# GpSimd's 1024 gathers of expert rows: a loop with copied lists of four ids, and one gather after the other that reads its own column of ids

## The chip, the cores and the metric

The kernel runs on one core of one Trainium2 chip. Its time is the device time of one launch in microseconds (us). Engines are named PE (TensorE, matmuls; PEld is its weight load), DVE (VectorE), ACT (ScalarE), POOL (GpSimd) and SP (SyncE, which only issues DMAs here). All DMAs, those of SP and those of POOL, run on the core's 16 DMA engines.

## The reference, cut to what matters

A decoder trunk of two layers on 256 tokens of 1024 numbers, all in float32. Each layer has a mixer (gated linear attention in layer 0, attention with forget gates in layer 1) and then a feed-forward part that looks up experts:

```python
def peer_ffn(xn, w_pq, sub_keys, u_tab, v_tab):
    q = einsum('td,de->te', xt, w_pq).reshape(T, 8, 2, 128)
    s = einsum('thcd,hcnd->thcn', q, sub_keys)
    s_top, i_top = lax.top_k(s, 16)
    cand = s_top[:, :, 0, :, None] + s_top[:, :, 1, None, :]
    best, pos = lax.top_k(cand, 16)             # 8 heads x 16 experts for each token
    ids = ...                                   # number of an expert, 0 to 16383
    gates = softmax(best)
    u = take(u_tab, ids)                        # one row of 1024 numbers each
    a = gelu(einsum('cd,chkd->chk', x, u))
    v = take(v_tab, ids)
    out = einsum('chk,chkd->cd', gates * a, v)
```

So every token needs 128 rows of the table u and 128 rows of the table v in each layer. With 256 tokens and 2 layers that is 2 x 2 x 128 gathers of u (one row for each of 128 tokens, 512 KB) and as many of v: 1024 gathers.

## The kernel before, in words

The tokens are two tiles (b = 0, 1) of 128, a token in each partition. A **phase** is the expert work of one layer and one tile; there are four, in the order (layer 0, tile 0), (0, 1), (1, 0), (1, 1). Each engine has one program, written out by hand, and semaphores join them. The mixers and the routing of the next phase are put between the experts of the phase that runs, in a fixed order on each engine.

The expert rows pass through two rings of SBUF, `u_ring` and `v_ring`, with 8 slots each (`RING`). A **round** fills both rings once, so a phase has 16 rounds, and a round has two **halves** of four slots. POOL issues an indirect DMA for each slot (L522 for u, L539 for v). It reads one id in each partition and fetches the row with this number.

For every u slot DVE multiplies the row with the token and sums it up (L796, a custom operation of two inputs, 128x1024), and so frees the slot (`u_free`). For a half ACT then computes the gelu (L1099), the weights (L1104) and for six of the eight slots a diagonal matrix (L1112). PE multiplies this diagonal with the v row and adds it up in PSUM (L1501, two matmuls of 128x512 a slot, `v_free`). The other two slots of v (2 and 3) are added by DVE (L806, `vec_free`).

SP loads the weights of the mixers and of the routing in blocks of 1 MB, nearly all into two places that take turns. A place can be loaded again only when PE has multiplied its last block (`w_used`). PE works in order: if it waits for a block of weights, the diagonals of the next experts wait behind that.

POOL's own program, after some constants, is the loop over rounds. In the function `turn` it takes four slots at a time (`ISSUE`): it waits until all four slots of u are free, copies the four ids of each token from `ids` to the small list `u_ids` (L516), waits for this copy (`ids_laid`) and issues four gathers of u; then the same for v with `v_ids` (L533). The loop's register picks the ids, while the gathers read at fixed addresses. A quarter of a phase (four rounds) begins when DVE has routed its two heads (`routed`).

Of the kernel before, what the change touches and what calls it, by code (L numbers as in the profile page):

```python
# [7 lines left out]
U32 = mybir.dt.uint32  # L8
# [5 lines left out]
P = 128  # L14
# [12 lines left out]
SLOTS = RH * RTOP  # L27

RING = 8
SUB = 4  # L30
ISSUE = 4
ROUNDS = SLOTS // RING
VEC_SLOTS = [2, 3]
PE_SLOTS = [j for j in range(RING) if j not in VEC_SLOTS]
VEC = len(VEC_SLOTS)
QUARTER = ROUNDS // 4
HALVES = ROUNDS * RING // SUB
LAST_VEC = RING - 3
PHASES = [(layer, b) for layer in range(2) for b in range(TILES)]
# [175 lines left out]
def yoco_kernel(nc, a, out):  # L215
# [9 lines left out]
    with ExitStack() as ctx:  # L225
        def sb(name, shape, dt=F32):
            return ctx.enter_context(nc.sbuf_tensor(name, shape, dt))

        def sem(name):
            return ctx.enter_context(nc.semaphore(name))  # L230
# [9 lines left out]
        u_ring = sb("u_ring", [P, RING, D])  # L240
        v_ring = sb("v_ring", [P, RING, D])
# [49 lines left out]
        ids = sb("ids", [P, TILES, SLOTS], U32)  # L291
# [1 line left out]
        gate_e = sb("gate_e", [P, SLOTS])  # L293
        gate_sum = sb("gate_sum", [P, RH])
        gate_inv = sb("gate_inv", [P, RH])
        u_ids = sb("u_ids", [P, RING], U32)
        v_ids = sb("v_ids", [P, RING], U32)
        dots = sb("dots", [P, RING])
        gelus = sb("gelus", [P, RING])
        weights_s = sb("weights_s", [P, RING])  # L300
# [48 lines left out]
        pv_full = sem("pv_full")  # L349
        queryT_full, queryT_ready = sem("queryT_full"), sem("queryT_ready")  # L350
        gate_x_ready, gate_e_ready, routed = sem("gate_x_ready"), sem("gate_e_ready"), sem("routed")
        ids_laid = sem("ids_laid")
        issued = sem("issued")
        u_loaded = [sem(f"u_loaded{j}") for j in range(RING)]
        v_loaded = [sem(f"v_loaded{j}") for j in range(RING)]

        u_free, v_free, vec_free = sem("u_free"), sem("v_free"), sem("vec_free")
# [33 lines left out]
        def multiplied(key):  # L391

            return w_used, RELEASE_OF[key] + 1
# [70 lines left out]
        def _(pool):  # L464
# [40 lines left out]
            u_rows = a["peer_u"].rearrange("l n d -> (l n) d")  # L505
            v_rows = a["peer_v"].rearrange("l n d -> (l n) d")

            def turn(ph, b, r, waits=None):

                for j0 in range(0, RING, ISSUE):  # L510
                    numbers = ids[:, b, bass.ds(r * RING + (j0 - ph * SLOTS), ISSUE)]
                    slots = range(j0, j0 + ISSUE)
                    n_laid = 2 * (j0 // ISSUE)
                    pool.wait_ge(u_free, r * RING + (j0 + ISSUE))
                    pool.sem_inc(issued, 1)
                    nc.gpsimd.tensor_copy(u_ids[:, j0:j0 + ISSUE], numbers).then_inc(ids_laid, 1)  # L516
                    if waits:
                        pool.wait_ge(*waits[n_laid])
                    pool.wait_ge(ids_laid, r * (2 * RING // ISSUE) + (n_laid + 1))
                    pool.sem_inc(issued, 1)  # L520
                    for j in slots:
                        pool.indirect_dma_start(  # L522
                            u_ring[:, j, :], None, u_rows, bass.IndirectOffsetOnAxis(ap=u_ids[:, j:j + 1], axis=0)
                        ).then_inc(u_loaded[j], 16)
                    on_pe = sum(j < j0 + ISSUE for j in PE_SLOTS)
                    on_dve = sum(j < j0 + ISSUE for j in VEC_SLOTS)
                    if any(j in PE_SLOTS for j in slots):
                        pool.wait_ge(v_free, r * len(PE_SLOTS) + on_pe)
                        pool.sem_inc(issued, 1)
                    if any(j in VEC_SLOTS for j in slots):  # L530
                        pool.wait_ge(vec_free, r * VEC + on_dve)
                        pool.sem_inc(issued, 1)
                    nc.gpsimd.tensor_copy(v_ids[:, j0:j0 + ISSUE], numbers).then_inc(ids_laid, 1)  # L533
                    if waits:
                        pool.wait_ge(*waits[n_laid + 1])
                    pool.wait_ge(ids_laid, r * (2 * RING // ISSUE) + (n_laid + 2))
                    pool.sem_inc(issued, 1)
                    for j in slots:
                        pool.indirect_dma_start(  # L539
                            v_ring[:, j, :], None, v_rows, bass.IndirectOffsetOnAxis(ap=v_ids[:, j:j + 1], axis=0)  # L540
                        ).then_inc(v_loaded[j], 16)

            for ph, (layer, b) in enumerate(PHASES):
                for quarter in range(4):
                    pool.wait_ge(routed, ph * 4 + quarter + 1)
                    first = ph * ROUNDS + quarter * QUARTER
                    if first == 0:

                        turn(0, 0, 0, [multiplied(key) for key in ((("wo", 0, 0), 2), ("r", 1),
                                                                   (("pq", 0, 0), 5), (("pq", 0, 0), 7))])  # L550
                    with pool.Fori(max(first, 1), first + QUARTER) as r:
                        turn(ph, b, r)


        @block.vector
# [1186 lines left out]
```

## Time and profile before

| what | value |
|---|---|
| median of 3 runs | 1933.5 us (1932.65 to 1946.42) |
| span of the profiled execution | 1954.8 us |
| instructions in it | 17629 |
| moved by DMA | 621.46 MB, of it 536.94 MB by the gathers |
| mean granted clock of PE | 0.835 of full speed |

The page of the profile gives no time of the profiled execution but its span, from the first instruction to the last, and the end of the output's DMA lies in it. The span is 21.3 us above the median of the runs and 8.4 us above the slowest of them. So an amount of time is taken off the span, and the difference is then carried over to the median.

To read it: time in which an engine is busy says what it does, and the waits say for whom. Where POOL neither works nor waits for another engine, the page puts the gap down to "issue". A gather's duration on POOL is the time in which POOL writes its descriptors; the rows land later, some 6 us after the issue.

### The profile page before, as it was taken

The page shows a single profiled execution, that of the slowest core. Times are in us where ns is not written, and L with a number is a line of the kernel's source. Part 1 is how long each engine was busy: PE and PEld are TensorE (multiplying, and loading weights), DVE is VectorE, ACT ScalarE, POOL GpSimd, SP SyncE. Part 2 cuts the span into 40 slices and gives each one's busy share as a digit, 9 for nine tenths or more (in the row PEclk, how much of TensorE's full clock was granted, in tenths as well). Part 3 has the DMA queues.
Part 4 walks back from the last instruction along what each step waited for, and adds up shares of the span by engine and source line. Part 5 has one row for each costly group of instructions (what it writes and reads, how often), then busy time and mean ns, then how long its engine had stood idle before and what let it go on. Part 6 is the DMA issues. An engine that isn't in the chain of part 4 may idle for free.

```text
span 1954.8 us, 17629 instructions
## 1 busy us (share of the span) xinstructions
PE 1344.8 (69%) x4795; PEld 799.3 (41%) x4800; DVE 1101.8 (56%) x2324; ACT 480.6 (25%) x1341; POOL 1239.8 (63%) x1317
## 2 busy tenths in 40 slices
PE   7997665566646868676846787698875766655554
PEld 6885322233313645444523454465442433222221
DVE  3336976544756539353574754834456588544445
ACT  3212233222212213242221212233122122211111
POOL 2007777775777755477577774745667777777774
PEclk9999887787878979878878898888887887878776
DMA  8459998999999997799998999977998999989997
GB/s 286 135 179 322 359 327 307 310 338 380 330 322 371 346 389 277 276 340 336 352 341 313 328 392 327 344 263 270 335 349 313 341 315 336 323 303 333 331 325 254
DMA packets 230275, 621.46 MB, mean 318 GB/s; under 512 B 21412, under 2 KB 97188, under 8 KB 230200
## 3 DMA queue, kind: packets, MB, share of 16 engines
q0 software_dynamic: 147456, 536.94, 76.3%
q1 hardware_dynamic: 82744, 83.62, 13.0%
q8 instruction: 36, 0.59, 0.1%
q14 instruction: 39, 0.32, 0.0%
HBM read 619.43 MB, written 1.05 MB: 317 GB/s over the span
## 4 chain that ended last, share of the span: by engine, by line
POOL 32%; issue 20%; PE 15%; DMA 14%; DVE 7%; ACT 2%; POOLq 1%; DVEq 0%; SPq 0%; ACTq 0%; PEldq 0%
POOL v_ring L539 16%; POOL u_ring L522 13%; PE acc L1501 8%; DMA u_ring<-in_peer_u,u_ids 4%; DVE u_ring L796 3%; DMA narrow<-in_kv_w 3%; PE pair L1350 3%; DMA wbuf<-in_fox_w_q 3%; DMA wbuf<-in_fox_w_o 2%; DVE h L806 2%; PE pair L1339 2%; POOL u_ids L516 1%; DMA wbuf<-in_gla_w_o 1%; DMA wbuf<-in_kv_w 1%; POOL v_ids L533 1%
## 5 line engine op out<-in xcount | busy, mean ns | idle before, releaser
L1501 PE MATMUL acc<-v_ring,diag 128*128 128x512 f32 x1524 | 826.5, 700 | 464.2 <-ACT diag L1112 462.5
L796 DVE CUSTOM_DVE_ANT_0 u_ring<-u_ring,xn 128x1024 f32<-128x1024 f32 x512 | 612.3, 1223 | 524.7 <-DMA u_ring<-in_peer_u,u_ids 520.6
L539 POOL DMA_INDIRECT v_ring<-in_peer_v,v_ids x512 | 598.3, 1169 | 223.2 <-issue 121.0
L1501 PEld LDWEIGHTS acc<-v_ring,diag 128*128 128x128 f32 x1524 | 334.3, 227 | 911.4 <-issue 618.5
L522 POOL DMA_INDIRECT u_ring<-in_peer_u,u_ids x512 | 540.8, 1056 | 225.8 <-issue 121.2
L1099 ACT ACTIVATE gelus<-dots 128x4 f32<-128x4 f32 x128 | 26.3, 205 | 865.1 <-DVE dots L796 864.7
L806 DVE SCALAR_TENSOR_TENSOR h<-v_ring,weights_s,h 128x1024 f32<-128x1024 f32 x128 | 164.4, 1284 | 32.2 <-ACT weights_s L1104 26.0
L1350 PE MATMUL pair<-wbuf,xT 128*128 128x256 f32 x352 | 98.1, 444 | 54.2 <-DMA wbuf<-in_kv_w 25.1
L516 POOL COPY u_ids<-ids 128x4 uint32 (+1 forms) x128 | 49.4, 386 | 126.8 <-DVE gates L737 126.1
L1112 ACT ACTIVATE diag<-ident,weights_s 128x128 f32<-128x128 f32 x381 | 125.3, 391 | 6.8
L533 POOL COPY v_ids<-ids 128x4 uint32 (+1 forms) x128 | 37.6, 294 | 120.3 <-PE acc L1501 110.9
L1099 ACT ACT_TABLE_LOAD x42 | 53.9, 1283 | 244.0 <-DVE dots L796 243.9
L1104 ACT ACTIVATE weights_s<-gelus,gates 128x1 f32<-128x1 f32 x512 | 109.0, 283 | 8.3 <-ACT gelus L1099 3.1
L1350 PEld LDWEIGHTS pair<-wbuf,xT 128*128 128x128 f32 x352 | 78.4, 227 | 75.9 <-DMA wbuf<-in_kv_w 28.0
L1339 PE MATMUL pair<-xT,wbuf 128*128 128x128 f32 (+2 forms) x528 | 79.6, 318 | 32.1 <-DMA wbuf<-in_fox_w_q 31.0
L1339 PEld LDWEIGHTS pair<-xT,wbuf 128*128 128x128 f32 (+1 forms) x528 | 73.4, 211 | 41.6 <-DMA wbuf<-in_fox_w_q 33.0
L1421 PEld LDWEIGHTS pair<-xT,wbuf 128*128 128x128 f32 x768 | 87.5, 192 | 6.3 <-issue 4.9
L1421 PE MATMUL pair<-xT,wbuf 128*128 128x128 f32 x768 | 87.8, 275 | 1.1 <-ACT xT L1032 1.1
L665 DVE TENSOR_TENSOR h<-h,pair 128x1024 f32<-128x1024 f32 x4 | 4.9, 1222 | 67.1 <-PE pair L1350 67.1
L796 DVE DVE_READ_ACCUMULATOR2_ANT dots<- 128x1 f32 x512 | 42.1, 82 | 0.0
L580 DVE SCALAR_TENSOR_TENSOR rows<-h,rstd,pair 128x1024 f32<-128x1024 f32 x4 | 5.1, 1281 | 55.1 <-PE pair L1405 55.0
L763 DVE TENSOR_REDUCE neg_max<-pair 128x2 f32<-128x256 f32 (+1 forms) x16 | 8.9, 558 | 46.7 <-PE pair L1458 46.6
(192 smaller groups left out, 1063.0 us busy)
## 6 DMA issues: line engine op xcount, KB each, us to landing
wbuf<-in_peer_w_q SPq DMA_DIRECT2D x20, 1024.0 KB, 14.9
wbuf<-in_kv_w SPq DMA_DIRECT2D x10, 1024.0 KB, 20.5
u_ring<-in_peer_u,u_ids POOLq DMA_INDIRECT x512, 6.2
v_ring<-in_peer_v,v_ids POOLq DMA_INDIRECT x512, 6.1
wbuf<-in_fox_w_q SPq DMA_DIRECT2D x8, 1024.0 KB, 16.6
wbuf<-in_fox_w_o SPq DMA_DIRECT2D x8, 1024.0 KB, 11.3
wbuf<-in_gla_w_o SPq DMA_DIRECT2D x6, 1024.0 KB, 15.0
wbuf<-in_gla_w_in SPq DMA_DIRECT2D x4, 1024.0 KB, 8.3
```

Source lines behind the costliest of these rows:

```text
L516: nc.gpsimd.tensor_copy(u_ids[:, j0:j0 + ISSUE], numbers).then_inc(ids_laid, 1)
L522: pool.indirect_dma_start(u_ring[:, j, :], None, u_rows, bass.IndirectOffsetOnAxis(ap=u_ids[:, j:j + 1], axis=0)).then_inc(u_loaded[j], 16)
L539: pool.indirect_dma_start(v_ring[:, j, :], None, v_rows, bass.IndirectOffsetOnAxis(ap=v_ids[:, j:j + 1], axis=0)).then_inc(v_loaded[j], 16)
L796: nc.vector.tensor_tensor_reduce(out=u_ring[:, j, :], in0=u_ring[:, j, :], in1=xn[:, b, :], scale=1.0, scalar=0.0, op0=ALU.mult, op1=ALU.a ...
L806: nc.vector.scalar_tensor_tensor(out=h[:, b, :], in0=v_ring[:, jv, :], scalar=weights_s[:, jv:jv + 1], in1=h[:, b, :], op0=ALU.mult, op1=A ...
L1099: nc.scalar.activation(gelus[:, s], dots[:, s], ACT.Gelu).then_inc(dots_free, 1)
L1104: ins = nc.scalar.activation(weights_s[:, j:j + 1], gelus[:, j:j + 1], ACT.Copy, scale=gates[:, b, bass.ds(r * RING + (j - ph * SLOTS), 1)])
L1112: nc.scalar.activation(diag[:, k, :], ident[:, :], ACT.Copy, scale=weights_s[:, j:j + 1]).then_inc(diag_ready, 1)
L1339: ins = nc.tensor.matmul(dst(m // P, mm), w[:, c, m:m + mm], x[:, c], start=(c == 0), stop=(c == KC - 1))
L1350: ins = nc.tensor.matmul(dst[:, i // 2, (i % 2) * WCOLS:(i % 2 + 1) * WCOLS], x[:, c, :], w[:, c, :], start=(c == 0), stop=(c == KC - 1))
L1421: ins = nc.tensor.matmul(dst[:, 0, o:o + P], w[:, c, m * P:(m + 1) * P], xT[:, slot, c, :], start=(c == 0), stop=(c == KC - 1))
L1501: ins = nc.tensor.matmul(acc[:, i, :], diag[:, k, :], v_ring[:, j, i * HALF:(i + 1) * HALF], start=False, stop=False)
```

## The change

Each of the 1024 gathers now stands by itself in POOL's program. Its ids come straight from a column of `ids` at a fixed address. The copies, the lists `u_ids` and `v_ids`, their semaphore and the loop are gone. Each gather waits for its own slot, where the loop waited for four slots at once. The order stays: four of u, four of v.

```diff
--- before.py
+++ after.py
@@ -28,7 +28,6 @@
 
 RING = 8
 SUB = 4
-ISSUE = 4
 ROUNDS = SLOTS // RING
 VEC_SLOTS = [2, 3]
 PE_SLOTS = [j for j in range(RING) if j not in VEC_SLOTS]
@@ -293,8 +292,6 @@
         gate_e = sb("gate_e", [P, SLOTS])
         gate_sum = sb("gate_sum", [P, RH])
         gate_inv = sb("gate_inv", [P, RH])
-        u_ids = sb("u_ids", [P, RING], U32)
-        v_ids = sb("v_ids", [P, RING], U32)
         dots = sb("dots", [P, RING])
         gelus = sb("gelus", [P, RING])
         weights_s = sb("weights_s", [P, RING])
@@ -349,7 +346,6 @@
         pv_full = sem("pv_full")
         queryT_full, queryT_ready = sem("queryT_full"), sem("queryT_ready")
         gate_x_ready, gate_e_ready, routed = sem("gate_x_ready"), sem("gate_e_ready"), sem("routed")
-        ids_laid = sem("ids_laid")
         issued = sem("issued")
         u_loaded = [sem(f"u_loaded{j}") for j in range(RING)]
         v_loaded = [sem(f"v_loaded{j}") for j in range(RING)]
@@ -505,51 +501,44 @@
             u_rows = a["peer_u"].rearrange("l n d -> (l n) d")
             v_rows = a["peer_v"].rearrange("l n d -> (l n) d")
 
-            def turn(ph, b, r, waits=None):
-
-                for j0 in range(0, RING, ISSUE):
-                    numbers = ids[:, b, bass.ds(r * RING + (j0 - ph * SLOTS), ISSUE)]
-                    slots = range(j0, j0 + ISSUE)
-                    n_laid = 2 * (j0 // ISSUE)
-                    pool.wait_ge(u_free, r * RING + (j0 + ISSUE))
-                    pool.sem_inc(issued, 1)
-                    nc.gpsimd.tensor_copy(u_ids[:, j0:j0 + ISSUE], numbers).then_inc(ids_laid, 1)
-                    if waits:
-                        pool.wait_ge(*waits[n_laid])
-                    pool.wait_ge(ids_laid, r * (2 * RING // ISSUE) + (n_laid + 1))
-                    pool.sem_inc(issued, 1)
-                    for j in slots:
-                        pool.indirect_dma_start(
-                            u_ring[:, j, :], None, u_rows, bass.IndirectOffsetOnAxis(ap=u_ids[:, j:j + 1], axis=0)
-                        ).then_inc(u_loaded[j], 16)
-                    on_pe = sum(j < j0 + ISSUE for j in PE_SLOTS)
-                    on_dve = sum(j < j0 + ISSUE for j in VEC_SLOTS)
-                    if any(j in PE_SLOTS for j in slots):
-                        pool.wait_ge(v_free, r * len(PE_SLOTS) + on_pe)
+            def u_group(ph, g):
+
+                b = PHASES[ph][1]
+                r, first = divmod(g * SUB, RING)
+                for j in range(first, first + SUB):
+                    at = r * RING + j - ph * SLOTS
+                    pool.wait_ge(u_free, r * RING + (j + 1))
+                    pool.indirect_dma_start(
+                        u_ring[:, j, :], None, u_rows, bass.IndirectOffsetOnAxis(ap=ids[:, b, at:at + 1], axis=0)
+                    ).then_inc(u_loaded[j], 16)
+
+            def v_group(ph, g):
+
+                b = PHASES[ph][1]
+                r, first = divmod(g * SUB, RING)
+                for j in range(first, first + SUB):
+                    at = r * RING + j - ph * SLOTS
+                    if j in VEC_SLOTS:
+                        pool.wait_ge(vec_free, r * VEC + (VEC_SLOTS.index(j) + 1))
+                    else:
+                        pool.wait_ge(v_free, r * len(PE_SLOTS) + (PE_SLOTS.index(j) + 1))
+                    pool.indirect_dma_start(
+                        v_ring[:, j, :], None, v_rows, bass.IndirectOffsetOnAxis(ap=ids[:, b, at:at + 1], axis=0)
+                    ).then_inc(v_loaded[j], 16)
+
+            for ph in range(len(PHASES)):
+                for g in range(ph * HALVES, (ph + 1) * HALVES):
+                    if g % (HALVES // 4) == 0:
+                        pool.wait_ge(routed, g // (HALVES // 4) + 1)
                         pool.sem_inc(issued, 1)
-                    if any(j in VEC_SLOTS for j in slots):
-                        pool.wait_ge(vec_free, r * VEC + on_dve)
+                    if g < 2:
+                        pool.wait_ge(*multiplied(((("wo", 0, 0), 2), (("pq", 0, 0), 5))[g]))
                         pool.sem_inc(issued, 1)
-                    nc.gpsimd.tensor_copy(v_ids[:, j0:j0 + ISSUE], numbers).then_inc(ids_laid, 1)
-                    if waits:
-                        pool.wait_ge(*waits[n_laid + 1])
-                    pool.wait_ge(ids_laid, r * (2 * RING // ISSUE) + (n_laid + 2))
-                    pool.sem_inc(issued, 1)
-                    for j in slots:
-                        pool.indirect_dma_start(
-                            v_ring[:, j, :], None, v_rows, bass.IndirectOffsetOnAxis(ap=v_ids[:, j:j + 1], axis=0)
-                        ).then_inc(v_loaded[j], 16)
-
-            for ph, (layer, b) in enumerate(PHASES):
-                for quarter in range(4):
-                    pool.wait_ge(routed, ph * 4 + quarter + 1)
-                    first = ph * ROUNDS + quarter * QUARTER
-                    if first == 0:
-
-                        turn(0, 0, 0, [multiplied(key) for key in ((("wo", 0, 0), 2), ("r", 1),
-                                                                   (("pq", 0, 0), 5), (("pq", 0, 0), 7))])
-                    with pool.Fori(max(first, 1), first + QUARTER) as r:
-                        turn(ph, b, r)
+                    u_group(ph, g)
+                    if g < 2:
+                        pool.wait_ge(*multiplied((("r", 1), (("pq", 0, 0), 7))[g]))
+                        pool.sem_inc(issued, 1)
+                    v_group(ph, g)
 
 
         @block.vector
```

In the order of POOL's program (row by row as it was compiled; ISA, REGISTER_ALU and the branch are steps of the sequencer) the body of the loop before reads, for the second half of a round and the end of the loop:

```order
L514 REGISTER_ALU
L516 ISA [waits u_free]
L516 COPY u_ids<-ids 128x4
L519 REGISTER_ALU
L522 DMA u_ring<-in_peer_u,u_ids 128x1024 [waits ids_laid]
L522 DMA u_ring<-in_peer_u,u_ids 128x1024 x3
L528 REGISTER_ALU
L533 COPY v_ids<-ids 128x4 [waits v_free]
L536 REGISTER_ALU
L539 DMA v_ring<-in_peer_v,v_ids 128x1024 [waits ids_laid]
L539 DMA v_ring<-in_peer_v,v_ids 128x1024 x3
```

One gather of four waits for a semaphore there, that of the copy. The changed program, at the beginning of a quarter of a phase, is:

```order
L511 DMA u_ring<-in_peer_u,ids 128x1024 [waits routed,u_free]
L511 DMA u_ring<-in_peer_u,ids 128x1024 [waits u_free] x3
L525 DMA v_ring<-in_peer_v,ids 128x1024 [waits v_free] x2
L525 DMA v_ring<-in_peer_v,ids 128x1024 [waits vec_free] x2
L511 DMA u_ring<-in_peer_u,ids 128x1024 [waits u_free] x4
L525 DMA v_ring<-in_peer_v,ids 128x1024 [waits v_free] x4
```

The gathers follow one another with nothing between them, and every one carries a wait for a slot. The programs of the other engines keep their instructions and their order.

## Rows read from the trace of the kernel before

**Rows 1.** The page, part 1: busy us, share, instructions of each engine.

```profile
PE 1344.8 (69%) x4795; PEld 799.3 (41%) x4800; DVE 1101.8 (56%) x2324; ACT 480.6 (25%) x1341; POOL 1239.8 (63%) x1317
```

**Rows 2.** POOL's groups by line: busy us, mean ns, idle before them and releasers.

```profile
L539 POOL DMA_INDIRECT v_ring<-in_peer_v,v_ids x512 | 598.3, 1169 | 223.2 <-issue 121.0 <-POOL v_ids L533 102.1
L522 POOL DMA_INDIRECT u_ring<-in_peer_u,u_ids x512 | 540.8, 1056 | 225.8 <-issue 121.2 <-POOL u_ids L516 103.1 <-PE acc L1501 1.5
L516 POOL COPY u_ids<-ids 128x4 uint32 (+1 forms) x128 | 49.4, 386 | 126.8 <-DVE gates L737 126.1
L533 POOL COPY v_ids<-ids 128x4 uint32 (+1 forms) x128 | 37.6, 294 | 120.3 <-PE acc L1501 110.9 <-DVE h L806 8.8
...
L498 POOL TENSOR_SCALAR_AFFINE_SELECT scratch<-scratch 128x128 f32<-128x128 f32 x7 | 4.5, 640 | 0.5
```

**Rows 3.** POOL in order of time: start us, us, what, idle before it.

```profile
1703.60 1.97 POOL L539 DMA_INDIRECT v_ring<-in_peer_v,v_ids  x1 [0.30 <-issue]
1705.57 0.39 POOL L516 COPY u_ids<-ids 128x4 uint32 x1
1706.77 0.96 POOL L522 DMA_INDIRECT u_ring<-in_peer_u,u_ids  x1 [0.81 <-POOL u_ids L516]
1708.03 0.94 POOL L522 DMA_INDIRECT u_ring<-in_peer_u,u_ids  x1 [0.30 <-issue]
```

**Rows 4.** DVE in order of time, beside the first of rows 3.

```profile
1703.54 1.22 DVE L796 CUSTOM_DVE_ANT_0 u_ring<-u_ring,xn 128x1024 f32<-128x1024 f32 x1
...
1704.69 1.22 DVE L796 CUSTOM_DVE_ANT_0 u_ring<-u_ring,xn 128x1024 f32<-128x1024 f32 x1
```

**Rows 5.** The line of u's gathers: durations in ns, least, median and most.

```profile
L522 POOL DMA_INDIRECT u_ring<-in_peer_u,u_ids x512: 935/941/1987, 143.5 to 1931.5; - x171
```

**Rows 6.** POOL's waits: us in total, times, longest us.

```profile
POOL v_ids L533 <- PE acc L1501: 110.9, 14, 20.3
```

**Rows 7.** The four phases: us, then PE, PEld, DVE, ACT, POOL busy, clock, DMA share, GB/s.

```profile
143.50:571.60 428.10, 268.38 (x866) 146.90 (x865) 271.61 (x576) 117.07 (x310) 304.93 (x320) 0.83 0.94 332
571.60:1047.00 475.40, 337.24 (x1264) 204.79 (x1265) 267.67 (x573) 121.30 (x354) 310.64 (x321) 0.83 0.92 335
1047.00:1524.50 477.50, 361.00 (x1359) 221.50 (x1360) 265.47 (x564) 119.91 (x338) 307.94 (x321) 0.84 0.90 325
1524.50:1938.40 413.90, 247.09 (x611) 114.25 (x612) 239.13 (x473) 79.22 (x273) 302.37 (x319) 0.80 0.92 325
```

**Rows 8.** The page, part 4: the chain that ended last, by engine.

```profile
POOL 32%; issue 20%; PE 15%; DMA 14%; DVE 7%; ACT 2%; POOLq 1%; DVEq 0%; SPq 0%; ACTq 0%; PEldq 0%
```

**Rows 9.** The chain in order of time: its longest pieces near where it leaves POOL.

```profile
394.68 5.25 DMA u_ring<-in_peer_u,u_ids
...
476.05 9.37 PE acc L1501 x16
...
657.36 5.58 DMA u_ring<-in_peer_u,u_ids
...
779.22 25.75 DMA wbuf<-in_fox_w_q
...
829.04 7.38 DMA u_ring<-in_peer_u,u_ids
...
1139.34 8.12 DMA u_ring<-in_peer_u,u_ids
```

**Rows 10.** The chain where it comes back to POOL.

```profile
817.46 1.17 POOL v_ids L533
```

**Rows 11.** POOL alone in the four stretches: us, busy (instructions), clock, share, GB/s.

```profile
394.70:485.60 90.90, 58.32 (x65) 0.79 0.98 357
657.40:817.50 160.10, 88.44 (x92) 0.85 0.89 325
829.00:956.60 127.60, 84.48 (x91) 0.80 0.97 348
1139.30:1434.70 295.40, 173.36 (x185) 0.84 0.89 323
```

**Rows 12.** Two windows of 50 us, columns as in rows 7.

```profile
200.00:250.00 50.00, 36.12 (x124) 20.16 (x124) 48.65 (x151) 12.25 (x34) 36.77 (x39) 0.86 0.97 353
600.00:650.00 50.00, 34.79 (x131) 19.95 (x130) 35.99 (x92) 13.79 (x33) 37.28 (x38) 0.83 1.03 391
```

## The prediction

> **What bounds the kernel now.** I read the busy shares first, then POOL's groups, POOL's rows in order of time, its waits, the windows of the four phases, and last the chain of waits. No engine is near full by the shares: PE has 69%, POOL 63%, DVE 56% [rows 1]. They mislead for POOL. Its gathers, copies and the gaps before them are 598.3 + 540.8 + 49.4 + 37.6 us of work and 223.2 + 225.8 us of gaps [rows 2], 1675 us in all, and the time from its first gather to its last is 1794.9 us (the sum of the four phases) [rows 7]. The gaps there are its own, "issue" or the wait for its own copy. What POOL waits for others is 110.9 us for PE in 14 places and 8.8 us for DVE (the 126.1 us for DVE's gates are the start, before the first gather) [rows 2, 6]. So outside of some 120 us POOL issues gathers as fast as it can, and the first question is how much of that is not gathering.
>
> The second question is where POOL matters for the end. The chain of waits gives POOL 32% and issue 20% of the span, and 38% to PE, DMA, DVE and ACT [rows 8]. In order of time the reader should see four long stretches in which the chain leaves POOL with a gather that lands, and goes through PE, DVE and blocks of weights, until PE frees a slot and POOL may go on: from 394.7 to 485.6, 657.4 to 817.5, 829.0 to 956.6 and 1139.3 to 1434.7 us [rows 9 to 11]. A block of weights alone is 25.75 us there [rows 9]. These are 674 us. In them POOL runs ahead of PE until its 8 slots are used up, and time saved on POOL is only waited out later. The other 1794.9 - 674 = 1121 us are led by POOL.
>
> **The change, part by part.** Work comes in 256 groups of four gathers (128 copies for u, 128 for v).
>
> *Removed: the copy.* On average it takes (386 + 294)/2 = 340 ns [rows 2].
>
> *Removed: the gap after the copy.* The gather behind it starts 0.81 us after its end. *Added in its place:* the gap between two gathers, 0.30 us [rows 3]. Together a group loses 0.34 + 0.81 - 0.30 = 0.85 us of about 6.5 us (1675/256), 217 us over all 256.
>
> *Added: a wait on every gather.* No row of before shows a gather that follows a gather and carries a wait. The bounds are 0.30 us (no wait, behind a gather) and 0.81 us (a wait, behind a copy) [rows 3]. I take 0.30. Semaphores by themselves are quick on POOL: the seven steps of L498, each of which waits for the one before, have 0.5 us of idle time together [rows 2], so most of the 0.81 is not the signal but the preparation of a gather that can't begin before the copy has ended. With a slot long free, nothing keeps the sequencer from preparing the next gather while the last one runs. Where the slot is not free the 0.81 appears, but the time is then PE's anyway.
>
> *Kept: the gather itself.* Its median is 0.94 us and its most 1.99 us [rows 5], with means of 1.169 and 1.056 [rows 2], so 0.17 us a gather come on top of the median. The row of 1.97 us lies under two operations of DVE that read two inputs each, and the one of 0.94 us at 1708 lies beside none [rows 3, 4]. I keep the 0.17, since DVE's work stays the same. The Trainium skill, "GPSIMD Engine Reference", section 1 (Specifications), says that POOL shares its interfaces to SBUF with VectorE and that instructions of VectorE with two SBUF inputs contend with it; by this rule the lengthening comes back with every gather, while one that came from full DMA queues would grow as POOL becomes faster. The rows fit the rule.
>
> *Removed: the loop, the waits for four slots at once.* The sequencer's steps run beside the gathers (the copy at 1705.57 starts right when the gather ends [rows 3]); I cost them at nothing. If that cover is missing it is a step of hundredths of a us each. A finer wait lets POOL start up to three slots earlier after a stall, at 14 places; PE then leads, and it gives nothing either.
>
> *Off and on the path.* In the four stretches POOL has 65 + 92 + 91 + 185 = 433 instructions, five to a group, 87 groups [rows 11]. Their 74 us become POOL's waits for PE. The other 169 groups lie on the path: 169 x 0.85 = 144 us. Two windows can't give their part. From 200 to 250 DVE is busy for 48.65 of 50 us (39/5 groups would save 6.6, at most 1.35 is there), and from 600 to 650 the DMA engines move 391 GB/s, the most of any window, with share 1.03 (6.5 us) [rows 12]. That leaves 144 - 5 - 7 = 132 us.
>
> **Sum.** 1954.8 - 132 = 1823 us for the span. The span is 21.3 us above the median of the runs; against that median of 1933.5 it is 1933.5 - 132 = 1801.5, so 1802 us. Its own range, from the unknown wait (0.36 us in place of 0.30 in half of the gathers is 30 us) and from stretches of PE that grow or shrink, is 1770 to 1835.
>
> What is late next: PE in the middle phases (337.24 of 475.4 us and 361.00 of 477.5 us busy [rows 7], 74% and 79% after the change), and the DMA engines elsewhere.
>
> **Rivals.**
>
> *All of it counts.* POOL's rows form a nearly closed line, and the chain may overstate PE: in the four stretches it is perhaps only just ahead, and the waits would stay at 120 us. Then all 217 us go: 1717 us. Against it speaks that the rings are only 8 slots deep and the chain does not touch POOL for up to 295 us [rows 11]. Chance 0.13, 1717 to 1770.
>
> *The DMA engines cap it.* In the last phase, with hardly any weights, they move 325 GB/s at a share of 0.92 [rows 7]; if the share can only go to 1, that is 353 GB/s. The last phase moves 413.9 x 325 = 134.5 MB, and needs 381 us, a gain of 33; the first moves 142.1 MB, 403 us, a gain of 25; the parts of the middle phases that POOL leads (188 and 182 us) gain 5%, 9 us each. Together 76 us: 1857 us. Against it: 391 GB/s over 50 us [rows 12]. For it: in that window a part are weights, and the share may count an idle wait as busy. Chance 0.18, 1835 to 1885.
>
> The Trainium skill, "DMA: Bandwidth & Descriptors", section Specifications, gives about 358 GB/s as a core's limit on HBM. With this figure the four gains would be 38, 31, 12 and 12 us, an estimate of 1840 us. The window of 391 GB/s stands against it as a limit for a core that runs alone.
>
> *Slower: each wait costs the long gap.* If 0.81 us belongs to any gather that carries a wait, and not to the copy, all 1024 have it. A gather is then 0.94 + 0.17 + 0.81 = 1.92 us, 1024 of them 1966 us, and POOL leads everywhere: with the 143.5 us before and the 16.4 us after them 2126 us of span, 2105 us as a median. It decides from a mean gap of 0.30 + 0.85/4 = 0.51 us upwards. For it: the only gathers with a wait have just this gap [rows 3]. Against it: the quick semaphores above. Chance 0.10, 1960 to 2110.
>
> *Nothing left.* Gathers that come sooner crowd the weights on the same 16 engines; if the blocks (25.75 us [rows 9]) take a third longer, the 674 us grow by what the rest gains. Chance 0.09, 1905 to 1960, in the main without a measurable difference. That the change does not do what it says is excluded by the compiled order: no copy is left between the gathers.
>
> **How the numbers follow.** My forecast has 0.50; with the cap (0.18) and all of it (0.13), faster by over 1% (1%, 19 us, is what a measurement of this kernel can tell) has 0.81. Same has 0.08 and slower 0.11, from the last two. The likeliest case gives 1802. The range has to hold 8 in 10: the forecast, the cap and most of the case above it, 1725 to 1890; outside are the two losing cases and the low end.
>
> **What would show it.** Right: gathers on POOL follow one another at 0.30 us, with means near 1.1 us; POOL's waits for PE grow from 111 to some 190 us; phases one and four shrink by about 40 and 50 us, the middle ones by 15 to 25 each; the windows of the last phase move about 370 GB/s. Wrong: a gap of 0.5 us or more before satisfied waits, gathers of 1.3 us in the mean without DVE beside them, a last phase that stays near 353 GB/s, or weights that land a third later.

## The result, and the profile after

The changed kernel takes 1799.3 us (median of 4 runs, 1787.6 to 1803.1), the kernel before 1933.1 us (4 runs on the same chip). The ratio is 0.928, with a 95% interval of 0.924 to 0.933: 134 us less. The forecast was 1802 us.

The page of the changed kernel, part 1 and part 4 (busy us by engine, then the chain that ended last):

```profile
PE 1304.0 (73%) x4800; PEld 789.3 (44%) x4800; DVE 1099.0 (61%) x2324; ACT 481.1 (27%) x1341; POOL 1167.7 (65%) x1061
...
PE 35%; POOL 21%; DMA 16%; DVE 16%; issue 9%; ACT 3%; DVEq 0%; SPq 0%; ACTq 0%; PEldq 0%; POOLq 0%
```

POOL has 256 instructions less. Its work falls from 32% of the chain [rows 8] to 21%, and "issue", of which most is POOL's but not all, from 20% to 9%. PE now has the largest part. The span is 1795.0 us, and the profiled run took 1796.7 us, so 1.7 us lie around a span. By this the execution of before that was profiled (1954.8 us) was some 23 us longer than a usual one; a difference between these two spans (160 us) is not the effect of the change.

POOL's groups by line (busy us, mean ns of one, idle before them):

```profile
L525 POOL DMA_INDIRECT v_ring<-in_peer_v,ids x512 | 588.7, 1150 | 322.8 <-PE acc L1490 189.0 <-issue 133.2 <-DVE h L795 0.7
L511 POOL DMA_INDIRECT u_ring<-in_peer_u,ids x512 | 565.4, 1104 | 286.0 <-issue 285.7 <-PEq L1418 0.3
```

The line of u's gathers, durations in ns (least, median, most), as [rows 5]:

```profile
L511 POOL DMA_INDIRECT u_ring<-in_peer_u,ids x512: 933/938/1993, 146.3 to 1772.1; - x171
```

The copies and the gaps behind them are gone. The gathers cost what they did: means of 1150 and 1104 ns against 1169 and 1056 [rows 2]. Of the 285.7 us of issue before u's gathers 130.2 us is the start of the program, ahead of the first one.

POOL's waits (us in total, times, longest):

```profile
POOL u_ring L511 <- issue: 285.7, 511, 130.2
POOL v_ring L525 <- PE acc L1490: 189.0, 78, 21.0
POOL v_ring L525 <- issue: 133.2, 433, 1.5
```

POOL in order of time in the last phase (start, us, what, idle before it):

```profile
1654.72 1.44 POOL L525 DMA_INDIRECT v_ring<-in_peer_v,ids  x1 [0.30 <-issue]
1656.46 0.95 POOL L511 DMA_INDIRECT u_ring<-in_peer_u,ids  x1 [0.30 <-issue]
1657.71 0.94 POOL L511 DMA_INDIRECT u_ring<-in_peer_u,ids  x1 [0.31 <-issue]
```

Every one of these gathers carries a wait, and the gap is still 0.30 us: (285.7 - 130.2)/510 and 133.2/433 give 0.305 and 0.308. What POOL waits for PE grew from 110.9 us in 14 places [rows 6] to 189.0 us in 78.

The four phases (us, then PE, PEld, DVE, ACT, POOL busy, clock, DMA share, GB/s):

```profile
146.30:531.70 385.40, 263.10 (x869) 146.31 (x868) 268.58 (x573) 117.17 (x310) 289.72 (x257) 0.84 0.98 368
531.70:966.40 434.70, 327.38 (x1264) 202.68 (x1264) 267.05 (x573) 119.86 (x346) 290.40 (x256) 0.86 0.98 366
966.40:1417.50 451.10, 348.63 (x1360) 217.85 (x1360) 265.77 (x570) 121.56 (x344) 290.20 (x257) 0.87 0.94 345
1417.50:1779.00 361.50, 231.71 (x612) 109.52 (x612) 239.44 (x475) 79.23 (x273) 283.76 (x256) 0.83 0.99 373
```

They are 43, 41, 26 and 52 us shorter than in the long execution of before [rows 7]. The last phase is the clearest: 256 gathers in 361.5 us are 1.41 us each. POOL's idle time in it, by what it waited for:

```profile
POOL u_ring L511 <- issue: 39.0, 128, 0.3
POOL v_ring L525 <- issue: 37.2, 122, 0.3
POOL v_ring L525 <- PE acc L1490: 1.8, 6, 0.3
```

That is 0.30 us in front of each gather and no longer wait. With 283.8 us of work it fills the phase, so POOL's own pace bounds it.

The chain in order of time (start us, us, what), its pieces where it leaves POOL or stays long with the weights:

```profile
409.49 25.17 DMA wbuf<-in_gla_w_o
...
602.75 16.33 DMA u_ring<-in_peer_u,ids
...
764.54 7.47 DMA u_ring<-in_peer_u,ids
...
1043.09 40.93 DMA wbuf<-in_kv_w
...
1428.93 5.96 DMA u_ring<-in_peer_u,ids
```

The stretches away from POOL are now 372 to 503, 602 to 755, 764 to 917 and 978 to 1369 us, 828 us in all, where they were 674 us [rows 11]. Stretches that POOL led by little have gone to PE and the weights. The chain also leaves POOL from 1429 to 1516 us, in the last phase, in which POOL never stood still for another engine; so a chain away from POOL is not yet proof that POOL has time to spare.

### The profile page after: what moved, and what is told of

Same layout as the page of the kernel before. It is cut to its first block, busy times and chain, and to the rows that moved or that the text cites. A ratio compares the mean times of both kernels' runs of the same rounds, so it can differ in the third digit from the quotient of the medians.

```text
span 1795.0 us, 15987 instructions
## 1 busy us (share of the span) xinstructions
PE 1304.0 (73%) x4800; PEld 789.3 (44%) x4800; DVE 1099.0 (61%) x2324; ACT 481.1 (27%) x1341; POOL 1167.7 (65%) x1061
## 4 chain that ended last, share of the span: by engine, by line
PE 35%; POOL 21%; DMA 16%; DVE 16%; issue 9%; ACT 3%; DVEq 0%; SPq 0%; ACTq 0%; PEldq 0%; POOLq 0%
PE acc L1490 15%; POOL v_ring L525 11%; POOL u_ring L511 10%; DVE u_ring L785 6%; PE pair L1339 5%; DMA u_ring<-in_peer_u,ids 4%; PE pair L1328 4%; DMA wbuf<-in_kv_w 4%; PE pair L1410 4%; DVE h L795 3%; DMA wbuf<-in_fox_w_o 3%; DMA wbuf<-in_fox_w_q 3%; PE acc L1339 2%; DMA narrow<-in_kv_w 1%; DMA wbuf<-in_gla_w_o 1%
## 5 line engine op out<-in xcount | busy, mean ns | idle before, releaser
L1490 PE MATMUL acc<-v_ring,diag 128*128 128x512 f32 x1524 | 780.3, 669 | 349.3 <-ACT diag L1101 347.3
L785 DVE CUSTOM_DVE_ANT_0 u_ring<-u_ring,xn 128x1024 f32<-128x1024 f32 x512 | 609.6, 1222 | 311.9 <-DMA u_ring<-in_peer_u,ids 306.9
L525 POOL DMA_INDIRECT v_ring<-in_peer_v,ids x512 | 588.7, 1150 | 322.8 <-PE acc L1490 189.0
L511 POOL DMA_INDIRECT u_ring<-in_peer_u,ids x512 | 565.4, 1104 | 286.0 <-issue 285.7
L1490 PEld LDWEIGHTS acc<-v_ring,diag 128*128 128x128 f32 x1524 | 319.9, 217 | 764.7 <-issue 549.2
L1339 PE MATMUL pair<-wbuf,xT 128*128 128x256 f32 x352 | 102.1, 456 | 60.4 <-DMA wbuf<-in_kv_w 26.5
L1010 ACT ACTIVATE square<-h 128x1024 bf16<-128x1024 f32 x10 | 10.5, 1053 | 88.0 <-DVEq L656 83.6
L661 DVE MAX8 top<-pair 128x8 f32<-128x128 f32 x64 | 14.2, 284 | 30.3 <-PE pair L1427 29.8
```

Source lines behind the costliest of these rows:

```text
L511: pool.indirect_dma_start(u_ring[:, j, :], None, u_rows, bass.IndirectOffsetOnAxis(ap=ids[:, b, at:at + 1], axis=0)).then_inc(u_loaded[j], 16)
L525: pool.indirect_dma_start(v_ring[:, j, :], None, v_rows, bass.IndirectOffsetOnAxis(ap=ids[:, b, at:at + 1], axis=0)).then_inc(v_loaded[j], 16)
L661: ins = nc.vector.max(vals[:, g, 0:8], src[:, g, :])
L785: nc.vector.tensor_tensor_reduce(out=u_ring[:, j, :], in0=u_ring[:, j, :], in1=xn[:, b, :], scale=1.0, scalar=0.0, op0=ALU.mult, op1=ALU.a ...
L1339: ins = nc.tensor.matmul(dst[:, i // 2, (i % 2) * WCOLS:(i % 2 + 1) * WCOLS], x[:, c, :], w[:, c, :], start=(c == 0), stop=(c == KC - 1))
L1490: ins = nc.tensor.matmul(acc[:, i, :], diag[:, k, :], v_ring[:, j, i * HALF:(i + 1) * HALF], start=False, stop=False)
```

## The experiments

Four of them ask where the 134 us come from. Their comparisons are with the kernel before on the same chip, at 1938 us.

**The loop alone** (e1). The gathers are written out, with copies and waits as before (the edit in short, against the kernel before):

```diff
-                    with pool.Fori(max(first, 1), first + QUARTER) as r:
-                        turn(ph, b, r)
+                for g in range(ph * HALVES, (ph + 1) * HALVES):
+                    group(ph, g, 0)     # waits for 4 slots, copies 4 ids, 4 gathers
+                    group(ph, g, 1)
```

> The gathers are written out without a loop, but with the copy of four ids and the wait for four slots before each group, as before. Removed is the loop alone. My theory: the loop costs nothing, the time is that of before, 1925 to 1940 us, and the gap after a copy stays 0.81 us. Rival 1 (the loop's branches and register steps are a cost of their own): 1880 us or less.

Measured: 1937.9 us, ratio 1.000 (0.997 to 1.003). The copy and its gap, by POOL's groups:

```profile
L546 POOL DMA_INDIRECT v_ring<-in_peer_v,v_ids x512 | 594.4, 1161 | 223.4 <-issue 118.5 <-POOL v_ids L532 103.6 <-DVE dots L812 1.2
...
L532 POOL COPY u_ids<-ids 128x4 uint32<-128x4 uint32 x128 | 49.1, 384 | 126.4 <-DVE gates L753 125.7
```

103.6 us behind 128 copies are 0.81 us again. The loop cost nothing that can be measured (the interval is 6 us to either side); the copies and what goes with them are all of the gain.

**The wait for four slots alone** (e2). No copies, but the first gather of a group waits for its four slots, in a step of its own (`sem_inc`) ahead of it, as in the kernel before (the edit in short, comments added):

```diff
-                    pool.wait_ge(u_free, r * RING + (j + 1))          # each gather
+                pool.wait_ge(u_free, r * RING + last)                 # first of four
+                pool.sem_inc(issued, 1)
```

> The changed kernel, but the first gather of a group waits until all four slots are free, as before, and the other three carry no wait. My theory: the finer wait gives next to nothing, since PE leads where it binds: 1795 to 1815 us, and the gaps between gathers are 0.30 us with and without a wait. Rival 2 (the finer wait carries a good part of the gain): 1830 us or more.

Measured: 1823.7 us (1816.0 to 1827.8), ratio 0.942 (0.936 to 0.948). That is a miss of both expectations, outside of mine by 9 us and short of the rival's 1830. The gaps are as expected, but the finer wait is worth something: the change has a ratio of 0.928 (0.924 to 0.933), and the next kernel, on the same chip as this one, 1798.1 us. POOL's waits in e2:

```profile
POOL v_ring L546 <- PE acc L1517: 197.8, 32, 28.8
POOL v_ring L546 <- issue: 150.1, 474, 4.7
POOL v_ring L546 <- DVE h L822: 20.2, 6, 12.2
```

Before gathers of v it waits 28 us more for PE and DVE than the change does (218.0 against 189.7). Two things can make this: a group of v that waits for its fourth slot keeps three free slots empty and holds back the u gathers behind it, and, as is shown below, POOL starts later after a wait that stands in its own step. Against e1 the copies alone, with the gap behind them, are worth 1937.9 - 1823.7 = 114 us.

**The copies where PE leads** (e3) and **where POOL leads** (e4). The changed kernel, with copy and wait for four slots put back in a part of the 256 groups:

```diff
+PE_LED = [range(39, 52), range(77, 95), range(97, 115), range(143, 179)]
+COPIED = lambda k: any(k in s for s in PE_LED)          # e3; "not any" in e4
...
+                if copied:
+                    nc.gpsimd.tensor_copy(lst[:, first:last], ids[:, b, at:at + SUB]).then_inc(ids_laid, 1)
```

> The changed kernel with the copies (and the wait for four slots) put back in 85 of the 256 groups, those that lay in the four stretches in which the chain of before ran through PE and the weights (groups 39 to 51, 77 to 94, 97 to 114, 143 to 178). My theory: these copies are waited out, so 85 x 0.85 = 72 us of POOL's time cost at most 15 us: 1797 to 1815 us. Rival 3 (all of POOL's time counts alike, 134 us for 256 groups, 0.52 us a group): 1799 + 44 = 1843 us.

> The changed kernel with the copies put back in the other 171 groups. My theory: they carry the whole gain, so it is close to before: 1910 to 1935 us. Rival 3 (0.52 us for each group): 1799 + 89 = 1888 us.

Measured: e3 1798.1 us (1794.1 to 1803.8), ratio 0.928 (0.923 to 0.934), the same as with no copy at all. e4 1937.2 us, ratio 1.001 (0.998 to 1.004), the same as before, and 2 us above the expected range. So the copies and coarse waits of 85 groups cost nothing that can be measured, and those of 171 cost everything, (1937.2 - 1798.1)/171 = 0.81 us a group. This is not the price of the copy alone: it has the wait for four slots in it, which by e2 is some 25 us. The rival that all of POOL's time counts alike (1843 and 1888 us) is out on both sides. In e3 the copies eat into POOL's waits:

```profile
POOL v_ids L533 <- PE acc L1518: 85.5, 13, 21.7
POOL v_ring L547 <- POOL v_ids L533: 34.0, 42, 0.8
POOL u_ring L547 <- POOL u_ids L533: 33.2, 41, 0.8
POOL v_ring L547 <- PE acc L1518: 27.1, 34, 10.9
```

POOL waits 113 us for PE there, where the changed kernel waits 189: 76 us less, close to the 85 x 0.85 = 72 us of work that was put in. Where the finer wait matters stays open. These 85 groups wait for four slots and lose nothing, which points at the other 171; but by the starts of the gathers e2 loses 15 of its 25 us in groups 143 to 178, which are among the 85 (303.7 us there, 288.8 in the changed kernel, 286.0 in e3).

**A filler between the groups** (e8) tests what the 0.81 us was:

```diff
+                pool.wait_ge(padded, pads)          # the memset before, long done
+                nc.gpsimd.memset(pad[:, :], 0.0).then_inc(padded, 1)
```

> The changed kernel with a small memset of 0.2 us put ahead of each group of four gathers. Nothing waits for it but the next memset. Theory A (the 0.81 us after a copy is the preparation of a gather, exposed because the gather waits for the copy): the gap between the memset and the gather stays near 0.30 us, so a group grows by 0.2 us, and 171 groups on the path give 34 us at most: 1800 to 1835 us. Theory B (any other instruction between gathers brings the long gap): the gap is 0.8 us, a group grows by 0.7 us, and the time is 1900 us or more.

Measured: 1817.7 us (1810.1 to 1822.3). In order of time:

```profile
1603.30 0.94 POOL L524 DMA_INDIRECT u_ring<-in_peer_u,ids  x1 [0.31 <-issue]
1604.24 0.22 POOL L513 MEMSET pad<- 128x128 f32 x1
1604.62 0.94 POOL L539 DMA_INDIRECT v_ring<-in_peer_v,ids  x1 [0.17 <-POOL pad L513]
```

The gap behind the memset is 0.17 us, less than behind a gather and than the 0.30 us expected. An instruction between gathers is cheap (0.22 + 0.17 - 0.30 = 0.09 us), and theory B is out. Theory A holds in that the wait brings the 0.81 us, but it is not the copy, nor waiting as such. In the kernel before, the wait for the copy does not stand on the gather: `wait_ge` is followed by `sem_inc(issued, 1)`, and this step of its own waits ahead of the gather (the compiled order before the prediction shows the two as one). e2 has no copy but such a step, and there a gather starts 0.81 us after DVE's second operation here has ended:

```profile
220.95 2.66 DVE L822 SCALAR_TENSOR_TENSOR h<-v_ring,weights_s,h 128x1024 f32<-128x1024 f32 x2
...
224.42 1.14 POOL L546 DMA_INDIRECT v_ring<-in_peer_v,ids  x1 [1.34 <-DVE h L822]
```

In the changed kernel the gather carries its wait itself, and starts 0.25 us after the DVE operation that it waited for (the first line is from the chain of waits):

```profile
1139.28 1.21 DVE h L795
...
1140.74 1.93 POOL L525 DMA_INDIRECT v_ring<-in_peer_v,ids  x1 [0.67 <-DVE h L795]
```

Over the whole traces, where POOL had stood still for over 0.4 us in front of a gather, the medians are 0.81 us at 37 places in e2 and 0.27 us at 51 places in the changed kernel, for PE and DVE alike. So the long gap belongs to a wait in a step of its own ahead of the gather. Two things follow, both untested. At e2's 37 places the later start is 37 x 0.54 = 20 us, an estimate that is near its 24 us, beside the slots kept empty. And a kernel that keeps the copies but puts the wait for them on the gather should get back some 0.54 of the 0.84 us of a group.

**What bounds the changed kernel: bytes or POOL's pace?** A DMA share of 0.98 to 0.99 looks like the engines' limit. Half rows (e6, one run; e12, four):

```diff
-                        u_ring[:, j, :], None, u_rows, bass.IndirectOffsetOnAxis(ap=ids[:, b, at:at + 1], axis=0)
+                        u_ring[:, j, 0:HALF], None, u_rows, bass.IndirectOffsetOnAxis(ap=ids[:, b, at:at + 1], axis=0)
```

> The changed kernel, each gather fetching only 512 of the 1024 numbers of a row; the other half of each slot is left as it was. 268 MB less go through the DMA engines, while POOL has the same gathers. If POOL's pace bounds the last phase, it stays at 355 to 365 us although the DMA share falls from 0.99 to below 0.6, and the whole time falls only by faster weights, to 1740 to 1790 us. If the DMA engines bound it (share 0.99), the last phase falls below 340 us, and the whole to less than 1720 us.

> The changed kernel, each gather fetching only 512 of the 1024 numbers of a row, timed over several rounds. If POOL's pace bounds the stretches outside PE's (a gather of 0.94 + 0.30 + 0.17 us), the last phase stays at 350 to 365 us and the whole at 1740 to 1795 us, PE's stretches being shorter by faster weights. If the DMA engines had a part in the changed kernel's time, as they have in the kernel with one input (1754 us with whole rows, 1628 us with half), the last phase falls below 340 us and the whole below 1720 us. If the single look (1810 us) was typical: 1800 to 1815 us.

Measured: 1810.0 us, and 1819.1 us (1808.0 to 1830.1), with 268 MB less. The last phase of e12:

```profile
1418.30:1796.50 378.20, 236.39 (x611) 111.09 (x612) 237.57 (x473) 79.36 (x273) 290.09 (x256) 0.80 0.63 179
```

The share falls to 0.63 and the rate to 179 GB/s, and the phase takes 378.2 us in place of 361.5: far from the 340 us of the theory of bytes, and also above the 365 us of the other. Gathers are a little longer here, 1231 and 1074 ns, for a reason that stays open. So bytes do not bound the last phase; POOL does. The whole time missed both theories: the expected drop of 10 to 60 us by faster weights did not come. How far bytes matter to the changed kernel outside its last phase is not shown by this. The changed kernel itself was not timed beside e6 or e12, which ran on two different chips, and on the chip of e6 another kernel took 149 us longer than elsewhere (e5, next). On the chip of e9 and e10 half the bytes did save time.

**What lengthens a gather** (e5, one run; e10, four). DVE's operation on a slot of u reads one input, and is as long (1214 ns against 1222):

```diff
-                    nc.vector.tensor_tensor_reduce(
-                        out=u_ring[:, j, :], in0=u_ring[:, j, :], in1=xn[:, b, :], scale=1.0, scalar=0.0,
-                        op0=ALU.mult, op1=ALU.add, accum_out=dots[:, j:j + 1]).then_inc(u_free, 1)
+                    nc.vector.tensor_reduce(dots[:, j:j + 1], u_ring[:, j, :], AX_X, ALU.add).then_inc(u_free, 1)
```

> The changed kernel with DVE's operation on a slot of u replaced by a sum over the row, which reads one input of 128x1024 in place of two and is about as long; the product with the token is left out. Theory A (what lengthens a gather on POOL is a DVE operation of two inputs beside it): the gathers' mean falls from 1.13 us to 0.98 us or less. Theory B (any long DVE operation beside it, or full DMA queues): it stays at 1.1 us or more.

> The kernel in which DVE's operation on a slot of u reads one input (the product is left out), timed. If its single look was typical: 1890 to 1915 us. If that look was disturbed: 1800 us or less.

POOL's groups in e10:

```profile
L525 POOL DMA_INDIRECT v_ring<-in_peer_v,ids x512 | 508.9, 994 | 430.3 <-PE acc L1488 318.2 <-issue 107.6 <-DVE h L793 4.5
L511 POOL DMA_INDIRECT u_ring<-in_peer_u,ids x512 | 498.1, 973 | 282.9 <-issue 249.7 <-DVE dots L785 33.2
```

The gathers' mean falls from 1.13 to 0.98 us. In e10's trace 391 gathers lie beside the sum over one input alone, and the longest of them takes 0.95 us; theory B is out. The edit takes away more than an input, though: the product was also written back, 128x1024, and the sum is not. The trace of the changed kernel speaks against this second cause. DVE's last addition of a phase writes as much, but reads only `h` from SBUF and `acc` from PSUM, and a gather that lies wholly beside it is short:

```profile
546.72 1.22 DVE L807 TENSOR_TENSOR h<-h,acc 128x1024 f32<-128x1024 f32 x1 [3.45 <-PE acc L1500]
...
546.86 0.93 POOL L511 DMA_INDIRECT u_ring<-in_peer_u,ids  x1 [0.31 <-issue]
```

The five gathers that lie beside such an addition, wholly or in part, take 933 to 938 ns. So it is the two inputs from SBUF: theory A. The Trainium skill, "GPSIMD Engine Reference", section 1, has this rule (contention with VectorE instructions of two SBUF inputs), and this case shows its price, 0.14 us a gather. The time was 1903.2 us in the one run of e5 and 1754.2 us (1749.9 to 1755.9) in the four runs of e10, the same kernel on another chip. The four runs stand; what delayed e5 stays open.

**Both together** (e9): one input and half rows.

> DVE's sum over one input (the product is left out) together with gathers of half a row. The kernel with one input alone took 1903 us, although its gathers were 0.13 us shorter, with POOL waiting 400 us for PE. Theory A (POOL at 1.24 us a gather runs ahead of the DMA engines, which need 1.3 us for 512 KB; the backlog delays what is needed first): with half the bytes the loss goes, the last phase takes 256 x 1.24 = 317 to 335 us, and the whole at most 1750 us. Theory B (the loss comes from DVE's own changed operation or from the order of the waits): the last phase stays above 360 us and the whole above 1850 us.

Measured: 1628.4 us, in one run. Here are the last phases of e10 and of e9:

```profile
1395.00:1736.00 341.00, 235.10 (x617) 111.53 (x615) 238.61 (x349) 79.35 (x273) 253.51 (x256) 0.81 1.01 397
```

```profile
1282.50:1613.50 331.00, 228.67 (x612) 109.20 (x612) 236.11 (x346) 78.72 (x271) 252.51 (x256) 0.83 0.71 204
```

With gathers of 0.98 us the DMA engines reach 397 GB/s over a whole phase, and half the bytes save 126 us in all (1754.2 to 1628.4). From the first gathers of each, the phases give 16, 47, 52 and 10 us of it. Most lies in the middle ones, which have the weights: a block of `in_kv_w` lands 10.6 us after its issue in e9 and 18.9 us in e10. In the last phase of e10 POOL's own pace, 253.5 us of work and 0.30 us in front of each gather, makes 331 of the 341 us. So 397 GB/s is the most that a phase moved, and not shown to be the engines' limit. The expectation's reason, a backlog that made e5 slow, fell with e5's own time.

**One input and a filler** (e11) was to test that reason.

> DVE's sum over one input (the product is left out), and a memset of 0.2 us ahead of each group of four gathers, which gives POOL back part of the time that it saved. Theory A (a pace of POOL above that of the DMA engines loses time): faster than with one input alone by 20 us or more, below 1885 us. Theory B (POOL's pace has no part in the loss): the same 1890 to 1915 us or slower.

Measured: 1761.1 us, 7 us above e10. Both theories had started from 1903 us; against e10's 1754 there is no loss to win back, and POOL's 0.09 us a group are hidden for the most part.

**u one group ahead** (e7): in a quarter of a phase the group of u is issued before the previous group of v.

```diff
-                    u_group(ph, g)
...
+                    elif (g + 1) % (HALVES // 4):
+                        u_group(ph, g + 1)
...
                     v_group(ph, g)
```

> The changed kernel with the groups of u issued one group earlier, ahead of the group of v that may wait for PE (not across the beginning of a quarter of a phase). Theory A (a v gather that waits for PE holds back the u gathers behind it, and DVE then waits for u): 10 to 30 us faster than the change, 1770 to 1790 us. Theory B (PE leads there anyway and needs v, not u): 1795 to 1810 us.

Measured: 1895.7, 1908.7, 1929.4 and 1938.2 us; from the lower two the ratio to the kernel before is 0.981 (0.974 to 0.989). Neither theory. A wait that neither had is in the trace, which is that of the longest run:

```profile
POOL u_ring L511 <- DVE dots L790: 233.1, 43, 30.2
```

Both rings hold two groups. Group g + 1 of u needs the slots of group g - 1, so POOL stands still until DVE has used these, with its routing in between, and the v gathers that PE needs stand behind. This explains a loss. Its size is open: the kernel ran on the chip on which e5 was slow, the changed kernel was not timed beside it, and its runs spread by 43 us.

## Why the prediction was right

*POOL's line and the price of a group.* Predicted 0.34 + 0.81 - 0.30 = 0.85 us; e1 has (384 + 282)/2 = 333 ns of copy and the same gaps, 0.84 us. Right. The 0.81 us a group of e4 against e3 is near it but measures something else, copy and coarse wait together.

*The unknown gap of a gather that carries a wait.* Taken at the low bound, 0.30 us; measured 0.305 and 0.308 us over 943 gathers. The rival that ends slower (0.81 us each, 2105 us) had a chance of 0.10 and is out. The reason given, that the 0.81 is not the signal but a preparation that can't begin before the wait is over, fits the filler, with 0.17 us behind a memset. But the prediction tied it to the copy and expected 0.81 us wherever a slot is not free; there the changed kernel has 0.27 us, because the wait stands on the gather and no longer in a step ahead of it.

*On and off the path.* 87 groups were costed at nothing, 169 in full. e3 and e4 split nearly the same groups, 85 and 171, and measured 0 and 139 us against the 0 and 144 of the sum. This was the step that made the number: without it the forecast is 1717 us. The idea is right; the 144 us are too much for the copies, as the next points show.

*The gather's lengthening stays.* 0.17 us by then, now (1150 + 1104)/2 - 940 = 187 ns. Right, and the cause is shown by e10.

*Two windows of DVE and DMA give nothing* (12 us). Not tested by itself. The cap on the DMA engines, the rival with 0.18, is refuted: the last phase moves 373 GB/s at a share of 0.99 (325 at 0.92 before [rows 7]), e10 397 GB/s, and in e12 half the bytes do not shorten it. (Its sum took 5% for POOL's part of the third phase too; from the 325 GB/s of that phase it would be 8%, some 5 us more.) To divide a rate by its share, as this rival did, gave a limit (353 GB/s) that does not exist; the Trainium skill's 358 GB/s ("DMA: Bandwidth & Descriptors", Specifications) is no limit for this core alone either.

*The finer wait gives nothing.* This step failed. e2 against the change is 24 us, 1.3%. "PE then leads, and it gives nothing either" looked only at the 14 stalls of before; in the changed kernel POOL stands still at 52 places for over 0.4 us, nine of them ahead of the first old stretch, and at 51 of them it starts again within 0.27 us.

*Against it.* The 24 us are not in the sum, and still the sum fits within 3 us. The term of the other sign is the copies: forecast at 132 us, measured at 114 (e1 against e2). That the two errors, 18 us too much and 24 too little, nearly cancel is luck; the range would have held either way. A likely reason for the 114 are the stretches that POOL does not lead, 674 us before and 828 us after, which the sum had let keep their length. This is an inference: no run takes it apart. The waits for PE grew by 78 us, as forecast (to 190).

*By phases.* Against e1, which is the kernel before in a usual execution (phases of 421.5, 467.0, 478.8 and 409.6 us, from the first gathers of each), the gains are 36, 32, 28 and 48 us. Predicted were about 40 and 50 for the outer ones and 15 to 25 for the middle ones. The middle ones gained more and the outer ones less than forecast.

*Span and median.* To carry the difference over to the median, 1933.5 - 132, and not to forecast from the long span, was needed: the difference of medians is 134 us, that of the two spans 160 us.

## What to carry to other kernels

When an engine is the bound by its own line, ask the chain of waits in which stretches it leads, and cost a saving only there: 85 of 256 equal savings were worth nothing here, and of the hoped-for 217 us the copies gave 114. A hit in the sum is no proof of its terms: the run that parts the two halves of a change (e2) found both mis-sized. A DMA share near 1 is no proof that bytes bound a phase; look at whether the issuing engine ever waits. In front of a gather look for a wait in a step of its own: it cost 0.81 us here, a wait on the gather itself 0.27 us, and a wait long met nothing.

## What the runs showed of the hardware

- A gather on POOL that follows a gather starts 0.30 us after its end, with or without a wait that is met; behind a memset that it does not wait for 0.17 us. After what it waited for has ended it starts 0.81 us later when the wait stands in a step of its own ahead of it (a copy in e1, PE and DVE in e2), and 0.27 us later when it carries the wait itself (51 places in the changed kernel).
- DVE operations with two inputs from SBUF beside a gather lengthen it from 0.94 to up to 1.99 us, on average by 0.17 us before and 0.19 us after; with one input in its largest operation the mean is 0.98 us, and beside an addition of one input from SBUF and one from PSUM gathers took 0.94 us.
- Gathers of 512 KB with 4 KB rows reached 397 GB/s over 341 us on this core, at a DMA share of 1.01, and the last phase of the changed kernel, at 373 GB/s and a share of 0.99, did not become shorter with half the bytes (378 against 361.5 us, on another chip).
- The same kernel (e5 and e10) took 1903 us in a single run on one chip and 1750 to 1756 us on another, while the kernel before differed between these chips by less than 1%.
